# The low parts of the even layer's weight units, made by VectorE in place of GpSimd

## The reference, cut to what matters

```
y = h @ w_in                                    # 528 x 1024 times 1024 x 2304
ys = y[..., :SHIFT_WIDTH]                       # 1792 columns = 14 tiles of 128
prev = jnp.pad(ys, ((0, 0), (1, 0), (0, 0)))[:, :L]
ys = ys + (prev - ys) * mu
r, k, v, wd, ad, gd = jnp.split(ys, RWKV_SPLITS, axis=-1)
wlog = -jax.nn.softplus(-(w0 + jnp.tanh(wd) @ w_up)) - 0.5
a = jax.nn.sigmoid(a0 + ad @ a_up)
g = jax.nn.sigmoid(gd) @ g_up
kk = k * k_k, normalized over each head of 64
kf = k * (1.0 + (a - 1.0) * k_a)
bonus = jnp.sum(r * kf * r_k, axis=-1) * v      # over each head
```

## Time and profile before

| what | value |
|---|---|
| runs, median (lowest to highest) | 3080.44 us (3078.55 to 3083.04) |
| the profiled execution's own time | 3083.83 us |
| its span | 3082.0 us |
| granted TensorE clock, mean | 0.97 |
| TensorE busy | 2844.6 us, 92% |
| VectorE busy | 1404.7 us, 46% |
| ScalarE busy | 998.1 us, 32% |
| GpSimd busy | 1093.5 us, 35% |

### The profile page before, as it was taken

The page is one execution under the profiler, slowest core; times in us unless marked ns, Lnnn a source line. Parts: engine busy times, 40 slices in busy tenths (PEclk is TensorE's granted clock), DMA queues, the critical chain, the costliest instruction groups (busy, mean ns, idle before and its releaser), DMA issues.

```text
span 3082.0 us, 45053 instructions
## 1 busy us (share of the span) xinstructions
PE 2844.6 (92%) x17982; PEld 2338.4 (76%) x17982; DVE 1404.7 (46%) x2210; ACT 998.1 (32%) x1524; POOL 1093.5 (35%) x773
## 2 busy tenths in 40 slices
PE   6888989989899999999989888899998999799997
PEld 4666567777688678787769877799998877678885
DVE  5788364610205621402128766480533447382452
ACT  3222354322212236523225433411123546332121
POOL 0233022344333159543433413244442321234442
PEclk9999999999999999999999998999999999999999
DMA  3889111244473259422222100222222210122222
GB/s 137 257 257 282 61 44 48 69 133 149 151 221 110 103 134 263 143 96 86 92 88 69 49 4 9 70 94 91 89 89 77 81 50 22 55 86 92 96 96 75
DMA packets 130750, 324.86 MB, mean 105 GB/s; under 512 B 54144, under 2 KB 54784, under 8 KB 129808
## 3 DMA queue, kind: packets, MB, share of 16 engines
q1 hardware_dynamic: 96128, 221.90, 21.5%
q0 software_dynamic: 30096, 88.21, 10.1%
q10 hardware_dynamic: 4352, 12.26, 1.0%
HBM read 288.32 MB, written 33.95 MB: 105 GB/s over the span
## 4 chain that ended last, share of the span: by engine, by line
PE 68%; DVE 18%; DMA 4%; ACT 4%; issue 3%; POOL 3%; DVEq 1%; ACTq 0%; SPq 0%; POOLq 0%
PE ps L270 17%; PE ps L273 17%; PE ps L275 17%; DMA d_pb<-arena 3%; POOL ring_r L363 2%; DVE h L603 1%; PE ps L925 1%; PE ps L1779 1%; PE ps L1520 1%; PE ps L583 1%; PE ps L280 1%; PE ps L1610 1%; PE ps L2194 1%; ACT high L372 1%; DVE inv L595 1%
## 5 line engine op out<-in xcount | busy, mean ns | idle before, releaser
L363 POOL TENSOR_TENSOR ring_r<-ring,high 128x1024 fp32r<-128x1024 f32 x335 | 829.2, 2475 | 1388.5 <-ACT high L372 1388.4
L270 PE MATMUL ps<-h_hi,high 128*128 128x512 f32 (+1 forms) x2104 | 736.9, 359 | 46.7 <-POOL ring_r L363 15.7
L275 PE MATMUL ps<-h_hi,ring_r 128*128 128x512 f32 (+1 forms) x2104 | 662.7, 350 | 0.0
L372 ACT ACTIVATE high<-ring 128x1024 fp32r<-128x1024 f32 x367 | 387.7, 1057 | 824.8 <-PE ps L270 697.2
L273 PE MATMUL ps<-h_r,high 128*128 128x512 f32 (+1 forms) x1912 | 644.5, 346 | 0.0
L270 PEld LDWEIGHTS ps<-h_hi,high 128*128 128x128 f32 x2104 | 400.6, 190 | 122.9 <-issue 48.6
L275 PEld LDWEIGHTS ps<-h_hi,ring_r 128*128 128x128 f32 x2104 | 371.3, 191 | 53.8
L273 PEld LDWEIGHTS ps<-h_r,high 128*128 128x128 f32 x1912 | 365.3, 191 | 41.9 <-issue 1.4
L273 PE MATMUL ps<-f_r,high 128*128 128x264 f32 (+1 forms) x960 | 295.7, 321 | 0.0
L270 PE MATMUL ps<-f_hi,high 128*128 128x264 f32 (+1 forms) x896 | 270.9, 317 | 2.1 <-POOL ring_r L363 1.8
L275 PE MATMUL ps<-f_hi,ring_r 128*128 128x264 f32 (+1 forms) x896 | 230.8, 316 | 0.0
(11 more groups left out here) (484 smaller groups left out, 4240.4 us busy)
## 6 DMA issues: line engine op xcount, KB each, us to landing
ring<-in_units SPq DMA_DIRECT2D x402, 512.0 KB, 3.3
d_ca<-arena POOLq DMA_DIRECT2D x16, 640.0 KB, 9.2
arena<-d_ca POOLq DMA_DIRECT2D x16, 640.0 KB, 6.9
arena<-d_q POOLq DMA_DIRECT2D x32, 256.0 KB, 8.2
d_pb<-arena POOLq DMA_DIRECT2D x16, 512.0 KB, 11.0
arena<-d_pb POOLq DMA_DIRECT2D x16, 512.0 KB, 4.0
arena<-d_ca POOLq DMA_DIRECT2D x16, 512.0 KB, 5.0
arena<-d_k POOLq DMA_DIRECT2D x128, 64.0 KB, 4.2
```

What stands on the lines that cost most here:

```text
L270: part = mm(acc, hi[:, cols], self.x_hi(k)[:, t0:t0 + tn], start=(k == 0), stop=False)
L275: ins = mm(acc, w[:, cols], self.x_hi(k)[:, t0:t0 + tn], start=False, stop=(k == self.kt - 1))
L363: eng.tensor_tensor(b.ring_r[:, slot, :], b.ring[:, slot, :], self.high[:, (j + self.flip) % 2, :], ALU.subtract).then_inc(b.unit_lo, 1)
L372: b.nc.scalar.activation(self.high[:, (j + self.flip) % 2, :], b.ring[:, u % RING, :], ACT.Copy).then_inc(b.unit_hi, 1)
```

## The change

VectorE takes the low parts over in this stage. In program order it makes that of unit 0 and unit 1 first; then, for every output `i`, that of unit `i + 1` ahead of the time shift and the preparation that belong to output `i`. `RwkvPrepare` has no GpSimd part any more. Nothing else is changed, neither the operation (`make_low`, L363) nor what TensorE, ScalarE and SyncE do and wait for.

```
-    def gpsimd(self, pool):
-        for i in range(len(EVEN_ORDER)):
-            g, n = self.out(i)
-            g.low_unit(pool, n)
-
     def scalar(self, act):
...
         at = col_at("ev_k_a_2")
         link(ts(m.rest_a, b.cols[:, at:at + 4], -1.0, 1.0, ALU.mult, ALU.add))
+
+        def low(i):
+            if i < len(EVEN_ORDER):
+                g, n = self.out(i)
+                g.low_unit(dve, n)
+
+        low(0)
         for i in range(len(EVEN_ORDER)):
+            low(i + 1)
             if i < len(self.shift.tiles):
                 self.shift.vector_tile(dve, i)
             j, part = divmod(i - 3, 3)
```

## The result

The changed kernel takes 3133.16 us (median of 4 runs, 3126.11 to 3137.07); the kernel before, run beside it, 3079.49 us. The ratio is 1.0175 (95% interval 1.0159 to 1.0192), 54 us more (49 to 59 by the interval). The prediction said 3130 in a range of 3112 to 3140.

A forecast was written before the change was run, and what follows sets the result against it. TensorE bounds the stage, with VectorE, slowed by GpSimd's low parts, pacing pairs 1 to 3. Unit 15 comes 38.7 us later; 8.4 and 2.4 of clock make 49.5, giving 3130 us, range 3112 to 3140.

The forecast's parts named there:

- The entry: Start of the stage: the first low part stands behind VectorE's norm work, so unit 1 begins 10.7 us late.
- P1 to P2: From P1's first matmul to P2's: 10.0 us with a 3.3 us TensorE stall; 8.5 and 1.8 in pair 0.
- P2 to the next P0: From P2's first matmul: 14.15 us, TensorE stalling 6.6 us for a low part behind VectorE's group, in four pairs.
- The loop without the clock: From P1 of pair 0 to unit 15: 116.7 us, a pair taking 31.35 us where it took 24.1.
- The clock: TensorE's lower clock after stalls: 8.4 us lost at four restarts of 2.1 each, 2.4 us in P2.
- the bound of 1.6 us: Clock loss in the half of P2 ahead of the bonus product: 0 to 1.6 us, 0.8 taken three times.
- The sum: Whole kernel: 38.7 + 8.4 + 2.4 = 49.5 us slower, predicted at 3130 us.
- the stalls of all three pairs: TensorE's stalls in pairs 1 to 3 before the change: 4.7 + 2.6 + 2.6 = 9.9 us, waiting for VectorE's `bonus_in`.
- the lock: VectorE operations beside a GpSimd low part take 2.78 us instead of 0.71: 2.07 us each, 6.2 us a pair.
- VectorE's work for a pair: VectorE in the loop: its work falls from 24.1 to 21.6 us a pair, beside TensorE's 21.5.
- half as much again as 8.4: Rival, longer waits: 12.4 us low clock at four restarts and 1.6 three times give 3136; chance 0.08 for above 3140.
- the locks set the pace and nothing takes their place: Rival, not slower: 9.9 us of stalls go in pairs 1 to 3, 10.7 come at the start: 3081.2 us; chance 0.04.

The follow-up runs named there:

- Experiment 1: The changed kernel, but GpSimd makes the low parts of units 0 and 1, VectorE the other 16: 3124.13 us, ratio 1.0145 to the kernel before.
- Experiment 2: The changed kernel, with the next P0's low part made ahead of VectorE's group at P1: 3100.24 us, ratio 1.0072 to the kernel before.
- experiment 6: Low parts two units ahead, GpSimd making the first two, next P1's low part moved inside VectorE's group at P1: 3068.12 us, ratio 0.9972 to the kernel before.
- experiment 5: Low parts two units ahead, GpSimd making the first two, plus 16 unused GpSimd subtractions: 3093.50 us, ratio 1.0050 to the kernel before.
- experiment 7: The changed kernel with unneeded matmuls filling TensorE's stalls: 32 per long stall 3127.93 us, 52 3122.08 us, 52 plus fillers ahead of P2 3120.79 us.

## Why the prediction was right

**The entry.** Said 10.7 us; from L713's start to P1 of pair 0 it is 32.24 us and was 21.20: 11.0. Experiment 1 gives 11.1.

**P1 to P2.** Said 10.0 us, 8.5 in pair 0; measured 10.06 three times and 8.62.

**P2 to the next P0.** Said 14.15; measured 14.27 and 14.29 in pairs 0 and 1. Experiment 2 shows the cause: the low part put ahead of the group removes the wait.

**The loop without the clock.** Said 116.7 us from P1 of pair 0 to unit 15; with all stalls filled, so that the clock stays up, 117.3.

**The clock.** Said 8.4 us at the four restarts; from P0's first matmul to P1's it took 8.7, 9.2 and 9.8 us and not 7.2, the last three units 19.6 and not 17.6: 8.1 together. Said 0.8 three times ahead of P2, 2.4 in all. Here a size was off: P2 to the next P0 took 14.3, 16.9 and 15.7 us in pairs 1 to 3, where 14.3 is the value at full clock, so 4.1 us. In pair 2 the low clock lasted through the whole first half of P2 and cost 2.6 us, beyond the bound of 1.6 us that I had set from a single row. The fillers confirm the sum of both: 127.7 - 117.3 = 10.4 up to unit 15 (the places above give 6.1 + 4.1), and 2.0 behind it.

**The sum.** 11.0 + 39.0 + 2.0 = 52.0 us in the stage, said 49.5; the medians differ by 53.7, and the 1.7 between are inside the interval. Of the missing 2.5 us 1.7 are P2's clock, 0.8 the loop without its clock (127.7 - 6.1 - 4.1 = 117.5) and 0.3 the entry; the restarts were 0.3 under. No term is large enough for the forecast to owe its number to errors that cancel.

**Pair 1 of the kernel before.** Here the prediction read too little. It saw the 0.93 of the stretch, but put the stalls of all three pairs down to the bonus product. In pair 1 that wait is 0.41 us, and the larger one stands ahead of the norm product and is for a sigmoid (the changed kernel has none there); behind it the clock fell:
```profile
1672.17 1.16 PE L1920 MATMUL ps<-sq,memn 128*128 128x264 f32 x4 [2.18 <-ACT arena L1991]
...
1672.90:1677.90 5.00, 4.86 (x26) 4.59 (x25) 4.89 (x5) 4.29 (x5) 2.87 (x1) 0.66 0.31 105
```
The sigmoid was late because VectorE was: its L1880 took 2.97 us at 1665.53, L2046 stands behind it, and ScalarE's square waited 3.33 us for L2046. So the lock is still the cause, but of the 4.7 us of pair 1 some 1.5 are the clock (the first half of P2 took 4.8 us, 3.3 in the pairs 2 and 3), after an idle time of only 2.18 us. That row was in the trace, and it warns that 0.8 us for each P2 could be too little. Two smaller slips move nothing: VectorE's work for a pair is 21.1 us if one starts from its busy 23.61 and not from the length 24.1 (measured 21.0), and half as much again as 8.4 is 12.6, not 12.4.

**The rivals.** That the locks set the pace and nothing takes their place was wrong for this order and right for another: nearly the same work on VectorE (16 of the 18 low parts, with the first two left on GpSimd), in the order of experiment 6, gives the 9.9 us that this rival counted. The condition that the prediction named for it, the low part of the next P0 ahead of the group at P1, was not enough. Experiment 2 was still 21 us slower than before; the entry is 11 of them, and P2's unit and then P1's were late as well. In the change as it was made the entry alone accounts for a fifth of the loss.

**The price on VectorE.** The Trainium skill's choice of VectorE for two-input work ("GPSIMD Engine Reference", section "4.1 Engine selection") held for the price, 1220 to 2603 ns. The price did not decide here: the 18 operations on VectorE cost 54 us in the order of this change, and 16 of them in the order of experiment 6 saved 9.5.

## What to carry to other kernels

Before work is moved to an engine that is faster at it, write down what stands ahead of it in that engine's program order and what that waits for: "one unit ahead" is one unit in the list, and no time at all when the operation in between waits for a product of the unit before. Put an operation that others wait for into the places where its engine waits itself; here four moved subtractions were worth 33 us. A long stall of TensorE is to be priced with the clock behind it: here 12 us in the loop and the last three units, on top of 40.

## What the runs showed of the hardware

- A GpSimd subtraction of 128x1024 numbers holds up a VectorE operation with two inputs for up to nearly all its length: by 2.07 us before and by 1.7 to 2.2 in experiment 5, where the two engines' tiles have nothing in common. For operations with one input the rows show both. VectorE's reciprocal L713 was no longer with GpSimd's low part beside it than without, 3.35 and 3.36 us; L2019 took 1.47 us beside one, and 0.43 in pair 2. In the trace before:
```profile
1643.99 2.41 POOL L363 TENSOR_TENSOR ring_r<-ring,high 128x1024 fp32r<-128x1024 f32 x1 [3.91 <-ACT high L372]
...
1645.23 1.47 DVE L2019 TENSOR_SCALAR arena<-arena 128x528 f32<-128x528 f32 x1 [1.57 <-ACT arena L1989]
```
- After 6.4 us without matmuls the clock was at the lower level at each of four restarts (first matmul 0.56 us and not 0.36). After 2.5 us in experiment 7 it was up at all four restarts and fell within 1.5 us behind three of them. After 3.0 us ahead of P2 the mean was 1.00 in one pair, 0.50 over 5.30 us in the next and 0.63 over 4.40 in the last. After 2.18 us in the kernel before it was 0.66 over 5.00 us, after 2.32 and 2.38 it stayed up. The length of the idle time alone does not tell what follows.
- Code that no edit touched gave places up to 10 us apart in twelve profiled executions. A difference of that size between two kernels is to be read from the stage, not from the span.
